# The MoE scatter as eight one-pass products with the bare one-hot, and the gathered tokens split by halves

## The reference, cut to what matters

```
for e in range(N_EXPERTS):
    y = swiglu(t, w_gate[e], w_up[e], w_down[e])        # 1024 -> 3584 -> 1024
    out = out + combine[:, e:e + 1] * y.astype(jnp.float32)
x = x + g2 * out
```

## Time and profile before

| | |
|---|---|
| profiled execution | 2958.59 us, span 2956.5 us, clock 0.985 |
| PE busy | 2844.1 us (96%), weight loads 2300.4 us (78%) |
| DVE busy | 1883.9 us (64%) |
| ACT busy | 1588.2 us (54%) |
| scatter, all turns (L1508) | 80 records in 10 groups of 8, median 592 ns |
| expert stretch, 950 to 1080 us | PE 129.05, DVE 110.86, ACT 93.69 of 130 us, DMA share 0.94 |

### The profile page before, as it was taken

One profiled execution on the slowest core, in us unless ns is written; L12 is line 12 of the kernel. 1 busy time (PEld: TensorE's weight loads), 2 busy tenths in 40 slices (PEclk: granted clock), 3 DMA queues, 4 the chain that ended last, 5 costly groups with the idle time before them and its releaser, 6 DMA issues. The chain is left out here.

```text
span 2956.5 us, 37763 instructions
## 1 busy us (share of the span) xinstructions
PE 2844.1 (96%) x14894; PEld 2300.4 (78%) x14895; DVE 1883.9 (64%) x2006; ACT 1588.2 (54%) x1879; POOL 20.1 (1%) x45
## 2 busy tenths in 40 slices
PE   6999999999999999999999999989999999999999
PEld 4779899778877878787787878767746997756798
DVE  3756555676597988888798888962633553352455
ACT  3574444566376777767677776752322443232344
POOL 0000000000000000000000000001000000000000
PEclk9999999999999999999999999999999999999999
DMA  9756444855579989898998989856233344413351
GB/s 339 265 170 244 171 172 142 300 169 184 209 284 352 339 322 364 328 363 327 341 347 328 364 325 368 325 188 217 98 110 114 143 171 150 165 57 142 118 202 72
DMA packets 311117, 693.77 MB, mean 235 GB/s; under 512 B 7254, under 2 KB 26180, under 8 KB 310996
## 3 DMA queue, kind: packets, MB, share of 16 engines
q1 hardware_dynamic: 309040, 689.07, 64.6%
q0 software_dynamic: 1344, 2.82, 0.4%
q10 hardware_dynamic: 612, 0.18, 0.0%
HBM read 690.99 MB, written 1.05 MB: 234 GB/s over the span
## 5 line engine op out<-in xcount | busy, mean ns | idle before, releaser
L2331 DVE TENSOR_TENSOR ring_rest<-ring,weights_hi 128x2048 fp32r<-128x2048 f32 x270 | 605.1, 2285 | 34.8 <-ACT weights_hi L1767 33.8
L1767 ACT ACTIVATE weights_hi<-ring 128x2048 fp32r<-128x2048 f32 x270 | 514.3, 1920 | 127.7 <-PE ps L1538 80.9
L1536 PE MATMUL ps<-weights_hi,xg_hi 128*128 128x512 f32 x1008 | 405.1, 402 | 3.3 <-DVE xg_lo L2331 3.3
L1538 PE MATMUL ps<-weights_hi,xg_lo 128*128 128x512 f32 x1008 | 397.4, 394 | 0.0
L1767 ACT ACTIVATE arena<-ps 128x512 f32<-128x512 f32 (+6 forms) x307 | 157.2, 529 | 329.5 <-PE ps L1132 119.9
L1537 PE MATMUL ps<-ring_rest,xg_hi 128*128 128x512 f32 x792 | 312.5, 395 | 0.0
L1767 ACT ACTIVATE arena<-arena 128x256 f32<-128x256 f32 (+5 forms) x309 | 152.9, 518 | 258.2 <-DVE arena L2331 163.9
L1555 PE MATMUL ps<-weights_hi,hidden_split_moe 128*128 128x512 f32 x1008 | 284.1, 393 | 0.0
L2331 DVE TENSOR_TENSOR w_split<-ring,w_split 128x1024 fp32r<-128x1024 f32 x128 | 150.8, 1221 | 165.9 <-ACT w_split L1767 165.9
L2331 DVE TENSOR_TENSOR late_rest<-arena,weights_hi 128x2048 fp32r<-128x2048 f32 x108 | 244.6, 2286 | 6.6 <-ACT weights_hi L1767 4.5
L1767 ACT ACTIVATE weights_hi<-arena 128x2048 fp32r<-128x2048 f32 x108 | 207.8, 1924 | 66.4 <-PE ps L1538 36.0
(11 more groups left out here) (247 smaller groups left out, 4873.5 us busy)
## 6 DMA issues: line engine op xcount, KB each, us to landing
ring<-in_moe_w_gate_dram SPq DMA_DIRECT2D x54, 2048.0 KB, 7.8
ring<-in_moe_w_up_dram SPq DMA_DIRECT2D x45, 2048.0 KB, 7.8
ring<-in_moe_w_down_dram SPq DMA_DIRECT2D x36, 2048.0 KB, 7.8
ring<-in_mlp_w_dram SPq DMA_DIRECT2D x32, 2048.0 KB, 7.7
arena<-in_moe_w_down_dram SPq DMA_DIRECT2D x27, 2048.0 KB, 7.9
ring<-in_w_mod_dram SPq DMA_DIRECT2D x48, 1024.0 KB, 9.2
ring<-in_w_in_dram SPq DMA_DIRECT2D x48, 1024.0 KB, 6.0
arena<-in_moe_w_up_dram SPq DMA_DIRECT2D x18, 2048.0 KB, 7.8
```

The source lines that it names most:

```text
L1536: pe.matmul(b, xg_hi[:, k, :], hi[:, i, :], start=(k == 0), stop=False)
L1538: mm = pe.matmul(b, xg_lo[:, k, :], hi[:, i, :], start=False, stop=(k == KD - 1))
L1767: return act.activation(o, i, func, **kw)
L2331: return dve.tensor_tensor(o, a, b, op)
```

## The change

The combine weight leaves the matrix. `to_tokens` still comes back from the transposes, but ACT's copy also sums each row into `slot_weight`, which is the weight of the slot's token. DVE then turns the matrix in place into a bare one-hot, `to_tokens_hot`, which is exact in the rounded format. `gated_y` multiplies with `slot_weight` as well. `y_slots` is split into `y_hi` (ACT) and `y_lo` (DVE), in halves of 512 columns, and the scatter is `hot` x `y_hi` plus `hot` x `y_lo`: eight fp32r products. The scatter keeps its place between gather and projections. The gathered tokens are rounded and split by halves, and ACT and DVE do their steps at the turn's start in a new order.

```diff
-                        done(pe.matmul(b, to_tokens[:, t * P:(t + 1) * P], y_slots[:, c * 512:(c + 1) * 512],
-                                       start=True, stop=True))
+                pe.wait_ge(sem("to_tokens_hot_ready"), 1 + e)
+                for i in range(2 * TT):
+                    t, c = i // 2, i % 2
+                    if t == 0:
+                        pe.wait_ge(sem("y_split_ready"), (c + 1) + e * 2)
+                    b = open_tile(i)
+                    hot, cols = to_tokens_hot[:, t * P:(t + 1) * P], slice(c * 512, (c + 1) * 512)
+                    pe.matmul(b, hot, y_hi[:, cols], start=True, stop=False)
+                    done(pe.matmul(b, hot, y_lo[:, cols], start=False, stop=True))
...
-                pe.wait_ge(sem("xg_split_ready"), 1 + e)
...
+                    if p < 2:
+                        pe.wait_ge(sem("xg_split_ready"), (p + 1) + e * 2)
...
+            def round_y(e):
+                for c in range(2):
+                    act.wait_ge(sem("y_gated"), (c + 1) + e * 2)
+                    f(y_hi[:, c * 512:(c + 1) * 512], y_slots[:, c * 512:(c + 1) * 512], ACT.Copy)\
+                        .then_inc(sem("y_rounded"), 1)
...
-                for p in range(4):
-                    round_piece(p)
+                round_piece(0)
+                round_piece(1)
+                round_y(e)
...
+                round_xg(0)
+                round_piece(2)
                 act.wait_ge(emptied["dve"], nth_at(lambda i: ("gather", i, 1), e))
-                f(xg_hi[:, :, :], xg, ACT.Copy).then_inc(sem("xg_rounded"), 1)
-                for p in range(4, HI_BUFFERS):
+                round_xg(1)
+                for p in range(3, HI_BUFFERS):
                     round_piece(p)
...
-                        f(to_tokens, acc(1, 0)[:, 0:T], ACT.Copy).then_inc(sem("to_tokens_ready"), 1)
+                        f(to_tokens, acc(1, 0)[:, 0:T], ACT.Copy, accum_out=slot_weight)\
+                            .then_inc(sem("to_tokens_ready"), 1)
...
+            def tokens_hot(e):
+                dve.wait_ge(sem("to_tokens_ready"), 1 + e)
+                ts(to_tokens_hot[:, :], to_tokens, 0.0, ALU.is_gt).then_inc(sem("to_tokens_hot_ready"), 1)
...
-                    ins = tt(y_slots[:, c * 512:(c + 1) * 512], acc(0, c), gb[:, 1, c * 512:(c + 1) * 512], ALU.mult)
-                ins.then_inc(acc_emptied, 1)
+                    stt(y_slots[:, c * 512:(c + 1) * 512], acc(0, c), slot_weight,
+                        gb[:, 1, c * 512:(c + 1) * 512], ALU.mult, ALU.mult).then_inc(sem("y_gated"), 1)
...
                 gated_y(piece_done(-1, e))
+                rest_of_y(e)
+                rest_of_xg(0)
                 dve.wait_ge(pe_done, step_at(lambda i: ("gather", i, 1), e))
...
                 add_scattered(0)
+                rest_of_xg(1)
                 add_scattered(1)
-                dve.wait_ge(sem("xg_rounded"), 1 + e)
-                tt(xg_lo[:, :, :], xg, xg_hi[:, :, :].bitcast(F32), ALU.subtract).then_inc(sem("xg_split_ready"), 1)
+                rest_of_piece(2)
                 add_scattered(2)
                 add_scattered(3)
...
+                    else:
+                        tokens_hot(e + 1)
```

More of the change, by code:

```diff
@@ L618, in program @@
         weighted = expert.cut(TT, P)
+        to_tokens_at = expert.pos
         to_tokens = expert.cut(T)
@@ L626, in program @@
         expert.cut(HI_BUFFERS, 2048)
+        y_hi, y_lo = rounded("y_hi", route_at, D), rounded("y_lo", y_at, D)
+        to_tokens_hot = rounded("to_tokens_hot", to_tokens_at, T)
+        slot_weight = sums[:, 0, 0:1]
         weights_hi = rounded("weights_hi", hi_at, HI_BUFFERS, 2048)
@@ L1500, in open_at, with scatter @@
                 return bank(key_of(0))
[L1502 to L1507, removed]
-                        done(pe.matmul(b, to_tokens[:, t * P:(t + 1) * P], y_slots[:, c * 512:(c + 1) * 512],
-                                       start=True, stop=True))
-            def wait_y(e):
-                pe.wait_ge(sem("to_tokens_ready"), 1 + e)
-                pe.wait_ge(acc_emptied, base_acc + 1 + e)
+            def scatter(open_tile, e):
+                pe.wait_ge(sem("to_tokens_hot_ready"), 1 + e)
[7 more added lines that the diff above has]
+                    done(pe.matmul(b, hot, y_lo[:, cols], start=False, stop=True))
             def expert_turn(e):
@@ L1543, in down @@
                     pe.wait_ge(sem("moe_rest_ready"), (p + 1) + e * n_pieces)
+                    if g == 0 and half == 0:
+                        pe.wait_ge(acc_emptied, base_acc + 1 + e)
                     if g < GROUPS - 1:
@@ L2142, in round_piece, with round_xg @@
                         .then_inc(sem("moe_rounded"), 1)
-                for p in range(4):
-                    round_piece(p)
+                def round_xg(half):
+                    f(xg_hi[:, 4 * half:4 * half + 4, :], xg[:, 4 * half:4 * half + 4], ACT.Copy)\
+                        .then_inc(sem("xg_rounded"), 1)
+                round_piece(0)
+                round_piece(1)
+                round_y(e)
                 act.wait_ge(pe_done, step_at(lambda i: ("gather", i, 0), e))
@@ L2838, in gated_y, with rest_of_y @@
                 for c in range(2):
-                    ins = tt(y_slots[:, c * 512:(c + 1) * 512], acc(0, c), gb[:, 1, c * 512:(c + 1) * 512], ALU.mult)
-                ins.then_inc(acc_emptied, 1)
+                    stt(y_slots[:, c * 512:(c + 1) * 512], acc(0, c), slot_weight,
+                        gb[:, 1, c * 512:(c + 1) * 512], ALU.mult, ALU.mult).then_inc(sem("y_gated"), 1)
+            def rest_of_y(e):
+                for c in range(2):
+                    dve.wait_ge(sem("y_rounded"), (c + 1) + e * 2)
+                    if c:
+                        dve.sem_inc(acc_emptied, 1)
+                    tt(y_lo[:, c * 512:(c + 1) * 512], y_slots[:, c * 512:(c + 1) * 512],
+                       y_hi[:, c * 512:(c + 1) * 512].bitcast(F32), ALU.subtract).then_inc(sem("y_split_ready"), 1)
             def expert_turn(e):
@@ L2861, in expert_turn, with rest_of_xg @@
                 rest_of_piece(1)
+                def rest_of_xg(half):
+                    dve.wait_ge(sem("xg_rounded"), (half + 1) + e * 2)
+                    tt(xg_lo[:, 4 * half:4 * half + 4, :], xg[:, 4 * half:4 * half + 4],
+                       xg_hi[:, 4 * half:4 * half + 4, :].bitcast(F32), ALU.subtract).then_inc(sem("xg_split_ready"), 1)
                 gated_y(piece_done(-1, e))
+                rest_of_y(e)
+                rest_of_xg(0)
                 dve.wait_ge(pe_done, step_at(lambda i: ("gather", i, 1), e))
@@ L2870, in expert_turn @@
                 add_scattered(0)
+                rest_of_xg(1)
                 add_scattered(1)
[L2872 to L2873 removed]
+                rest_of_piece(2)
                 add_scattered(2)
                 add_scattered(3)
[L2876 removed]
+                for p in range(3, HI_BUFFERS - 1):
                     rest_of_piece(p)
@@ L2906, in skipped @@
                 dve.sem_inc(acc_emptied, 1)
+                for name in ("y_gated", "y_split_ready"):
+                    dve.wait_ge(sem(name), e * 2)
+                    dve.sem_inc(sem(name), 2)
+                dve.wait_ge(sem("to_tokens_hot_ready"), 1 + e)
+                dve.sem_inc(sem("to_tokens_hot_ready"), 1)
             over_turns(dve, expert_turn, skipped)
@@ L2910, in _ @@
             gated_y(value["moe_down", TURNS - 1, GROUPS - 1])
+            rest_of_y(TURNS)
             for t in range(TT):
```

11 lines of the change are left out of this document (8 added, 3 removed).

## The result

| | median, us | lowest to highest | runs |
|---|---|---|---|
| before | 2954.39 | 2952.07 to 2954.69 | 4 |
| after | 2984.8 | 2980.84 to 2986.0 | 4 |

The ratio is 1.0092, with an interval of 1.0080 to 1.0103: the changed kernel is slower, by some 27 us (the two medians as they stand lie 30.4 us apart). Measured again later, beside another set of runs of the kernel before, it was 1.0070 (1.0056 to 1.0084), 21 us. The profiled execution took 2980.84 us (span 2978.7, clock 0.981), 22.2 more than that of before.

What follows compares the result with a forecast made beforehand. PE bounds each expert turn, with VectorE setting its waits at the seam. Stalls of 1.27 and 0.71 plus some clock loss gave 2.4 a turn, 9 x 2.4 = 21.6 us: 2980 profiled, 2976 as median, range 2966 to 2985.

Steps and rivals of the forecast that it cites:

- PE's own gain: Scatter at the seam between expert turns: eight one-pass products take 1.86 us instead of 3.4, saving 1.6 less a seam.
- Rival 4: Scatter: one-pass products cost 0.4 us each instead of 0.2325, moving the forecast by under 0.2 a turn; chance 0.06.
- p0 later by 1.27: Seam: the first weight piece's projection starts at 960.66 instead of 959.39, 1.27 us later, behind VectorE's late emptying and add.
- The sign that p0 would be released by the add: Seam, PE's rows: the first projection product would be released by VectorE's add, and no longer by xg_lo.
- The second stall of 0.71 at p8: First down piece: PE waits 0.71 us because VectorE finishes the rest of the rounded hidden tile late.
- The clock: Behind the seam's gaps: a 3.4 us low-clock spell costs 1.56 us; 1.98 to 2.83 a turn, 2.4 taken.
- rival 1: All nine seams lose the clock: 9 x 2.83 = 25.5 us, total 2980; chance 0.18.
- Mid-turn at nothing: Middle of a turn: tokens_hot (under 0.5 us) and ACT's accumulator read (0.19) cost nothing, 0.3 a turn if uncovered.
- The last scatter at nothing: Tenth scatter, after the last turn: costs nothing, with 3 us of cover from the final gain's transfer against 1.4.
- The split into halves at nearly nothing: Steps of 512 instead of 1024 elements: nearly no cost, or some 0.3 us a turn if steps don't overlap.
- Rival 2: Seam: gather half 1 emptied before 958.3, so p0 starts 0.55 to 1.2 us earlier; 2943 to 2949; chance 0.08.
- Rival 5: Only the first stall, as the cover before the first down piece holds: 9 x 1.27 = 11.4 us, 2966; chance 0.20.

Runs made afterwards that it cites:

- the lead of four: The changed kernel with VectorE's rests of the weight pieces taken four pieces ahead of PE instead of five: 2977.47 us, 1.0066 times the kernel before.
- gather half 1 first: The changed kernel, rests four pieces ahead, gather half 1 emptied before the rests of y and of the tokens: 2965.69 us, 1.0030 times the kernel before.
- the one-pass scatter alone: The changed kernel without halves: tokens split in one piece, gather half 1 emptied right behind the rests of y: 2969.72 us, 1.0037 times the kernel before.
- The one-pass kernel that is faster: The changed kernel, rests four pieces ahead, y gated before piece 1's rest, which moves behind the first add, ScalarE reordered: 2948.66 us, 0.9964 times before.

## Why the prediction was right

The forecast was 2976 us (2966 to 2985), slower; 2984.8 was measured, inside the range and near its top. Point by point:

- **PE's own gain.** Half as large as foretold: with 0.33 for a product that opens a tile and up to 0.44 between tiles the eight take 2.6 us, not 1.86, so PE saves some 0.8, not 1.6. (Nor do 72 products in 16.89 us make 0.2325 each, but 0.2346.) It does not stand in the sum, and it bought nothing, as the forecast said. Rival 4 (0.4 each) is refuted by the scatter in one go, 0.23 to 0.33.
- **p0 later by 1.27.** Measured 1.48 (9.85 against 8.37), on the chain that was foretold: emptying of gather half 1 behind the wait for `xg_hi`. 0.12 of the difference is the gating: scalar_tensor_tensor from PSUM takes 1.40 for two steps, where I had put the 1.28 of the old product. By the emptying's end the chain is 0.16 late, and 0.06 more come in the last hop to PE. The sign that p0 would be released by the add did not show: the row has no idle time, since the fourth pair takes 0.78 instead of 0.47 and ends just when the add could release p0. That both hang on the place of the emptying was shown by putting it back: 1.3 us.
- **The second stall of 0.71 at p8.** Measured 0.51 (6.55 against 6.04) at full clock, and shown to be VectorE's lead by the lead of four. It is smaller by what p0 is later: p8 itself starts 33.27 behind the gather, where the forecast had 33.28. At full clock VectorE's way to p8 sets the turn, and the two errors cancel. With a spell the stall is hidden, as foretold.
- **The clock.** Foretold: 1.98 a turn without a spell, 2.83 with one, the middle taken. Measured: 2.05 and 2.24, and 2.7 to 3.1 (mean 2.96), with spells in seven and in five of the nine seams. At 1.2 GHz a product takes 0.43, and a spell behind p0 makes T0 1.5 longer, both as foretold. The share of seams, half by the middle taken, was too low for the profiled execution. The stretch grew by 24.6 against 21.6 in the sum and 25.5 by rival 1 (all nine turns); that rival was nearer in the total, though two seams do not pay. The forecast set one gap that lost the clock against one that kept it; the trace of before has a third, of 2.46 too, and behind it the clock was down at 728.9:

```profile
728.16 0.38 PE L1176 MATMUL ps<-attn_hi,mix_hi 128*128 128x256 f32 x1 [2.46 <-DVE attn_lo L2331]
```

- **Mid-turn at nothing.** Right: `tokens_hot` takes 0.29 and stands in an idle stretch; no wait of PE inside a turn but p8. **The last scatter at nothing.** Right: VectorE still waits 3.49 us for the final gain behind it.

```profile
2007.73 0.77 PE L1515 MATMUL ps<-y_hi,to_tokens_hot 128*128 128x512 f32 x1 [4.20 <-DVE y_lo L2356]
...
2013.99 1.23 DVE L2356 TENSOR_TENSOR arena<-arena 128x1024 f32<-128x1024 f32 x1 [3.49 <-DMA arena<-in_final_gain_dram]
```

- **The split into halves at nearly nothing.** Right for the durations: back to back two rests of y take 1.47 at the first seam (the second starts 0.78 after the first, since it waits for ScalarE), and two adds 1.28 as before. The end kept for steps that don't overlap, 0.3 a turn, did not come.
- **Rivals 2, 3 and 5.** Rival 2 named the point from which it would be faster: gather half 1 emptied before 958.3. In the order of the change it ended at 960.86, which is 960.05 on the clock of that text (the gather started 0.81 later here), as it was worked out to within 0.16. But reaching this point is not enough, though the rival said it would be. With gather half 1 first it is emptied at 956.56 on that clock, and in the one-pass scatter alone at 958.09, and both kernels are slower than before. The one-pass kernel that is faster, 0.9964, also gates y before the rest of piece 1, so that the first tile does not wait. Rival 5 needed the second cover to hold; it did not at full clock.

Against the profiled run the sum said 2980, and it took 2980.84. That fit is partly luck: the stretch was under-sized by 3 us (more spells than the middle, and 0.2 at p0 where a spell hides the stall), and the rest of the program happened to be 2.4 shorter. Against the median the forecast is 9 low: I took off 4.3 for a profiled run above its median, and this time it was the fastest of four. The medians of before taken later, 2957.8 to 2958.93, lie where that profiled run lay, so the 4.3 was no property of the kernel.

What stays open: why the same two gaps lose the clock in one seam and keep it in the next. Filling them removed all the spells, and leaving more of them brought two a seam, so the gaps are the cause; what decides in between, no run here tells.

## What to carry to other kernels

A product made cheaper by splitting its operand puts a round trip (VectorE to ScalarE and back) in front of it. Before counting what PE saves, write down what stands in the order *behind* the waiting step on VectorE: here the emptying of a PSUM bank that the next tile and then the next projection needed, and it cost 1.3 us a turn against a saving of 0.8 that nobody was waiting for. Measure the parts of a change apart: one half of this one was a gain of 0.25%, hidden behind the loss of the other. A single step that looks like the culprit can be put right without a gain: with the emptying back in its place the kernel was still slower than before, because the next wait, for the rests of y, took over. And try the order of steps before the arithmetic: with the old scatter, order and halves alone gave 0.5% against the kernel before, and the cheaper products nothing on top that can be measured.

## What the runs showed of the hardware

- Two gaps of 1.43 and 1.94 us with 2 us of products between them lowered the granted clock to 1.2 GHz for 3.4 us behind six of eight seams in one execution, four of eight in another and three of eight in a third (the lead of four); one gap of 2.55 did so behind six of eight; gaps of 1.42 and 1.71 behind one; 0.59 and 0.74 behind none. With gaps of 0.68, 0.16, 0.82 and 2.17 and only single products between them it was 6.8 us behind six of eight. The rule of the Trainium skill ("Perfetto Trace Analysis", Matmul Optimizations) to run matmuls back to back is borne out, though two of nine seams kept the clock; products that compute nothing satisfied it, and were worth 0.9 us in a turn that would have had a spell.
- Less work on PE and VectorE can make a stretch longer: without four products and two VectorE steps a turn it took 1191.4 us against 1184.4.
- scalar_tensor_tensor from PSUM takes 1.40 us for two steps of 128x512 where the product of two operands takes 1.28.
- One-pass products of 512 columns that follow each other at 0.23 us in the projections take 0.33 where they open a tile and up to 0.44 between two tiles of the scatter. Why, no run here shows.
- At 1.2 GHz such a product takes 0.43 us.
